# Instruction streams of TensorE, ScalarE and VectorE put in order by a list scheduler

## The reference

```python
for i in range(2):
    n = rms_norm(h, g_mix[i])
    h = h + (conv_pair_mixer(n, ...) if i % 2 == 0 else chunked_sgu_mixer(n, ...))
    mem_n = rms_norm(mem, g_mem[i])
    h = h + memory_cross_attention(rms_norm(h, g_xattn[i]), mem_n, ...)
    h = h + swiglu(rms_norm(h, g_ffn[i]), ...)      # (silu(n @ w_gate) * (n @ w_up)) @ w_down, width 2816
return rms_norm(h, g_final)
```

## Time and profile before

| | |
|---|---|
| median of 3 runs | 1797.18 us (1795.05 to 1807.06) |
| the profiled execution's own time | 1793.89 us |
| its span on the slowest core (core 3) | 1792.4 us; the eight cores 1776.1 to 1792.4 us |
| busy: PE, DVE, ACT | 90%, 56%, 38% of the span |
| mean granted TensorE clock | 0.972 of full speed on core 3 |
| DMA | 130.60 MB, 73 GB/s on the mean |

### The profile page before, as it was taken

The page is one execution under the profiler, slowest core; times in us unless marked ns, Lnnn a source line. Parts: engine busy times, 40 slices in busy tenths (PEclk is TensorE's granted clock), DMA queues, the critical chain, the costliest instruction groups (busy, mean ns, idle before and its releaser), DMA issues.

```text
span 1792.4 us, 23249 instructions; the slowest of 8 cores (1776.1 to 1792.4 us)
## 1 busy us (share of the span) xinstructions
PE 1614.3 (90%) x7650; PEld 732.0 (41%) x7650; DVE 998.7 (56%) x1602; ACT 687.5 (38%) x1153; POOL 70.6 (4%) x147
## 2 busy tenths in 40 slices
PE   3899868899999989899997797989989999989995
PEld 1344433444334434344443354444433444434442
DVE  1539654645774356663555762554777346673555
ACT  3522364454362132531434432354445133342242
POOL 1000000000000000000000001000000000000000
PEclk9899988999999999999998899999999999999998
DMA  9152537430145354443430209032023445364332
GB/s 227 51 95 36 83 57 179 72 59 1 22 73 82 55 93 76 81 73 71 88 69 16 47 1 153 13 71 48 1 48 65 77 74 103 71 164 82 74 70 94
DMA packets 32373, 130.60 MB, mean 73 GB/s; under 512 B 3584, under 2 KB 10112, under 8 KB 25472
## 3 DMA queue, kind: packets, MB, share of 16 engines
q0 software_dynamic: 18432, 100.03, 32.3%
q1 hardware_dynamic: 13824, 29.08, 5.5%
HBM read 216.51 MB, written 8.39 MB: 125 GB/s over the span
## 4 chain that ended last, share of the span: by engine, by line
PE 69%; DVE 12%; ACT 7%; issue 6%; DMA 5%; SPq 1%; DVEq 0%; ACTq 0%; POOLq 0%
PE ps L487 53%; PE ps L485 13%; PE ps L80 2%; ACT L80 1%; DMA hT_63<-x_in 1%; DVE sw L80 1%; DMA wbuf_185<-w_od_out 1%; DVE wd L80 1%; DVE t_3_62 L80 1%; DVE nT_68 L80 1%; DVE t_2_61 L80 1%; PE ps L909 1%; DVE hT_65 L80 1%; DVE w_0_94 L80 1%; DVE w_4_98 L80 1%
## 5 line engine op out<-in xcount | busy, mean ns | idle before, releaser
L487 PE MATMUL ps<-pT,VW 128*128 128x512 f16 x512 | 122.0, 387 | 4.0 <-DVE pT L80 4.0
L80 ACT ACTIVATE ps<-ps 128x512 f32<-128x512 f32 x88 | 47.7, 567 | 179.2 <-PE ps L487 178.6
L80 DVE TENSOR_TENSOR hT_63<-hT_63,ps 128x512 f32<-128x512 f32 x64 | 44.0, 688 | 113.3 <-PE ps L487 112.9
L487 PE MATMUL ps<-tw,sw 128*128 128x512 f16 x352 | 84.4, 382 | 6.7 <-DVE sw L80 4.4
L485 PE MATMUL ps<-tw,sw 128*128 128x512 f16 x352 | 86.0, 387 | 4.2 <-ACT ps L80 3.5
L80 ACT ACT_TABLE_LOAD x42 | 53.9, 1283 | 69.2 <-PE ps L80 29.4
L80 DVE TENSOR_TENSOR hT_64<-hT_64,ps 128x512 f32<-128x512 f32 x64 | 43.9, 686 | 62.4 <-PE ps L487 62.1
L487 PEld LDWEIGHTS ps<-pT,VW 128*128 128x128 f16 x512 | 50.8, 100 | 67.4 <-issue 9.8
L80 ACT ACTIVATE pT<-ps,epsc 128x512 f16<-128x512 f32 x64 | 43.7, 683 | 77.0 <-PE ps L487 76.4
L80 DVE TENSOR_TENSOR hT_66<-hT_66,ps 128x512 f32<-128x512 f32 x64 | 43.8, 685 | 49.6 <-PE ps L487 49.4
L80 DVE TENSOR_TENSOR hT_65<-hT_65,ps 128x512 f32<-128x512 f32 x64 | 43.9, 686 | 49.3 <-PE ps L487 49.1
(11 more groups left out here) (1236 smaller groups left out, 3372.3 us busy)
## 6 DMA issues: line engine op xcount, KB each, us to landing
hT_64<-x_in SPq DMA_DIRECT2D x8, 512.0 KB, 17.4
hT_65<-x_in SPq DMA_DIRECT2D x8, 512.0 KB, 20.3
hT_66<-x_in SPq DMA_DIRECT2D x8, 512.0 KB, 18.2
X<-a_ph SPq DMA_DIRECT2D x16, 130.0 KB, 6.0
hT_63<-x_in SPq DMA_DIRECT2D x4, 512.0 KB, 10.5
yA<-yst SPq DMA_DIRECT2D x32, 64.0 KB, 6.5
out<-hT_63 SPq DMA_DIRECT2D x4, 512.0 KB, 5.9
out<-hT_64 SPq DMA_DIRECT2D x4, 512.0 KB, 3.3
```

Of the source, the lines that this page charges most:

```text
L80: return self.add(eng, lambda e: getattr(e, meth)(**kw), reads, writes)
L487: ins = e.matmul(out, lhsT=l, rhs=r, start=(i == 0), stop=(i == np_ - 1))
```

## The change

Recording stays as it is. Each operation now carries an estimate of its cost (`_op_cost`, `_mm_cost`, bytes for a DMA). Before the semaphores are assigned, `schedule` plays the program through with these costs, a latency per engine from an operation's end to its users (LAT), and one shared link for all DMAs at 190 KB per us, plus 0.8 us ahead of a transfer and 1.2 us after it. Each engine has a window of its next operations in recorded order (AHEAD: 6 on PE, 10 on ACT, 12 on DVE, 1 on POOL and SP). Step by step the operation of any window that can start earliest is taken, the earlier recorded one where two are equal, and it is appended to the engine's new stream. POOL and SP, with a window of 1, keep their order. No operation is added or taken away. Dependencies are kept per operation (`after`) and cut to the last one per engine only after the new order is known. Neither a load of ACT's function tables nor TensorE's clock is in the costs.

```diff
--- before.py
+++ after.py
@@ -55,7 +55,29 @@
         self.dead = False
 
 class Op:
-    __slots__ = ("eng", "fn", "deps", "idx", "need_inc", "dma", "dma_val")
+    __slots__ = ("eng", "fn", "deps", "after", "idx", "need_inc", "dma", "dma_val", "cost", "done", "users", "left",
+                 "ready", "n")
+
+def _free(ap):
+    n = 1
+    for s in ap.shape[1:]:
+        n *= s
+    return n
+
+def _op_cost(eng, kw):
+    aps = [v for k, v in kw.items() if k in ("out", "in_", "in0", "in1", "rhs", "ap") and hasattr(v, "shape")]
+    n = max(_free(a) for a in aps)
+    if eng == "pe":
+        return _mm_cost(n)
+    if eng == "act":
+        return 0.19 + n / 1200
+    if eng == "dve":
+        half = all("16" in str(a.dtype) for a in aps)
+        return 0.155 + n / (1920 if half else 960)
+    return 0.1 + n / 600
+
+def _mm_cost(n):
+    return max(0.025, n / 2400 + 0.0025)
 
 class Ring:
     def __init__(self, items):
@@ -69,30 +91,36 @@
 
 class Prog:
     ENGS = ("pe", "act", "dve", "pool", "sp")
+    AHEAD = {"pe": 6, "act": 10, "dve": 12, "pool": 1, "sp": 1}
+    LAT = {"pe": 0.25, "act": 0.08, "dve": 0.08, "pool": 0.1, "sp": 0.1}
+    DMA_RATE = 190e3
     EPOCH = 500
 
     def __init__(self):
         self.streams = {e: [] for e in self.ENGS}
         self.dma_cnt = {}
         self.final_dma = set()
+        self.count = 0
 
     def op(self, eng, meth, reads=(), writes=(), **kw):
-        return self.add(eng, lambda e: getattr(e, meth)(**kw), reads, writes)
+        return self.add(eng, lambda e: getattr(e, meth)(**kw), reads, writes, cost=_op_cost(eng, kw))
 
     def dma(self, eng, sem, reads=(), writes=(), **kw):
-        return self.add(eng, lambda e: e.dma_start(**kw), reads, writes, dma=sem)
+        return self.add(eng, lambda e: e.dma_start(**kw), reads, writes, dma=sem, cost=kw["in_"].nbytes())
 
     def dma_part(self, eng, sem, slot, first, reads=(), **kw):
         prev = slot.w
-        o = self.add(eng, lambda e: e.dma_start(**kw), reads, [slot] if first else [], dma=sem)
+        o = self.add(eng, lambda e: e.dma_start(**kw), reads, [slot] if first else [], dma=sem, cost=kw["in_"].nbytes())
         if not first:
             assert prev.dma == sem
             slot.w = o
         return o
 
-    def add(self, eng, fn, reads=(), writes=(), dma=None):
+    def add(self, eng, fn, reads=(), writes=(), dma=None, cost=0.1):
         o = Op()
         o.eng, o.fn, o.dma, o.need_inc, o.idx, o.dma_val = eng, fn, dma, False, None, None
+        o.cost, o.done, o.users, o.n = cost, None, [], self.count
+        self.count += 1
         deps = {}
         for s in reads:
             assert not s.dead, s.name
@@ -109,25 +137,84 @@
                 for r in v.r.values():
                     deps[id(r)] = r
         for s in reads:
-            s.r[eng if dma is None else ("dma", id(o))] = o
+            s.r[id(o)] = o
         for s in writes:
             s.w = o
             s.r = {}
         deps.pop(id(o), None)
-        o.deps = []
-        for d in deps.values():
-            if d.dma is None and dma is None and d.eng == "pe" and eng == "pe":
-                continue
-            o.deps.append(d)
-            if d.dma is None:
-                d.need_inc = True
+        o.after = list(deps.values())
         if dma is not None:
             self.dma_cnt[dma] = self.dma_cnt.get(dma, 0) + 16
             o.dma_val = self.dma_cnt[dma]
         self.streams[eng].append(o)
         return o
 
+    def schedule(self):
+        heads = {e: [] for e in self.ENGS}
+        rest = {e: iter(self.streams[e]) for e in self.ENGS}
+        out = {e: [] for e in self.ENGS}
+        free = {e: 0.0 for e in self.ENGS}
+        link = 0.0
+        for e in self.ENGS:
+            for o in self.streams[e]:
+                o.left, o.ready = len(o.after), 0.0
+                for d in o.after:
+                    d.users.append(o)
+
+        def fill(e):
+            while len(heads[e]) < self.AHEAD[e]:
+                o = next(rest[e], None)
+                if o is None:
+                    return
+                heads[e].append(o)
+        for e in self.ENGS:
+            fill(e)
+        while True:
+            best = None
+            for e in self.ENGS:
+                for o in heads[e]:
+                    if o.left:
+                        continue
+                    t = max(free[e], o.ready)
+                    if best is None or (t, o.n) < best[:2]:
+                        best = (t, o.n, e, o)
+            if best is None:
+                break
+            t, _, e, o = best
+            heads[e].remove(o)
+            out[e].append(o)
+            if o.dma is None:
+                free[e] = t + o.cost
+                o.done = free[e] + self.LAT[e]
+            else:
+                free[e] = t + (0.6 if e == "pool" else 0.1)
+                link = max(link, t + 0.8) + o.cost / self.DMA_RATE
+                o.done = link + 1.2
+            for u in o.users:
+                u.left -= 1
+                u.ready = max(u.ready, o.done)
+            fill(e)
+        assert all(len(out[e]) == len(self.streams[e]) for e in self.ENGS)
+        self.streams = out
+        return max(free.values())
+
     def assign(self):
+        for e in self.ENGS:
+            for i, o in enumerate(self.streams[e]):
+                o.n = i
+        for e in self.ENGS:
+            for o in self.streams[e]:
+                last = {}
+                for d in o.after:
+                    if d.dma is None and o.dma is None and d.eng == "pe" and e == "pe":
+                        continue
+                    key = d.eng if d.dma is None else ("dma", id(d))
+                    if key not in last or last[key].n < d.n:
+                        last[key] = d
+                o.deps = list(last.values())
+                for d in o.deps:
+                    if d.dma is None:
+                        d.need_inc = True
         neps = {}
         for e in self.ENGS:
             c = 0
@@ -486,7 +573,8 @@
                 else:
                     ins = e.matmul(out, lhsT=l, rhs=r, start=(i == 0), stop=(i == np_ - 1))
             return ins
-        o = self.P.add("pe", fn, reads=reads, writes=[self.ps_s[b]])
+        o = self.P.add("pe", fn, reads=reads, writes=[self.ps_s[b]],
+                       cost=sum(_mm_cost(_free(r)) for _, r in pairs))
         self.tick(np_ / KC)
         return o
 
@@ -631,7 +719,7 @@
                     ins = e.matmul(self.ps[b][:, i * NMEM:(i + 1) * NMEM], lhsT=ws[i][0](k), rhs=mn[:, k, :],
                                    start=(k == 0), stop=(k == KC - 1))
             return ins
-        P.add("pe", fn, reads=ws[0][1] + ws[1][1] + list(mn_s), writes=[self.ps_s[b]])
+        P.add("pe", fn, reads=ws[0][1] + ws[1][1] + list(mn_s), writes=[self.ps_s[b]], cost=16 * _mm_cost(NMEM))
         self.tick(1)
         P.op("act", "activation", [self.ps_s[b]], dst_s[2 * mp:2 * mp + 2],
              out=dst[:, 2 * mp:2 * mp + 2, :].rearrange("p m n -> p (m n)"), in_=self.ps[b][:, :], func=AF.Copy)
@@ -856,7 +944,7 @@
                         ins = e.matmul(ps[:, cc * 128:(cc + 1) * 128], lhsT=self.v_ln[tt][:, cc, g * 128:(g + 1) * 128],
                                        rhs=self.w_sT[:, g, :], start=True, stop=True)
                     return ins
-                P.add("pe", fn, reads=self.v_ln_s[tt] + [self.w_sT_s], writes=[self.ps_s[bs]])
+                P.add("pe", fn, reads=self.v_ln_s[tt] + [self.w_sT_s], writes=[self.ps_s[bs]], cost=4 * _mm_cost(128))
                 bu = self.linear(self.wc("od_in", 0, g), KC, lambda k: self.nT[tt][:, k, :], self.nT_s[tt], TT)
                 ug = self.t32.next()
                 P.op("act", "activation", [self.ps_s[bu]], [ug.slot], out=ug.t[:, :], in_=self.ps[bu][:, :],
@@ -910,7 +998,7 @@
                                        lhsT=w(c), rhs=self.kT[:, c, :],
                                        start=(hc == 0), stop=(hc == 1))
                 return ins
-            P.add("pe", fn, reads=ws + self.kT_s[4 * hp:4 * hp + 4], writes=[self.ps_s[b]])
+            P.add("pe", fn, reads=ws + self.kT_s[4 * hp:4 * hp + 4], writes=[self.ps_s[b]], cost=4 * _mm_cost(NMEM))
             self.tick(1)
             evict(b, self.G[:, d, hp * 512:(hp + 1) * 512], self.G_s[d])
 
@@ -1179,6 +1267,7 @@
         assert not self.reserved, self.reserved
         dma_names = sorted(self.P.dma_cnt.keys())
         with ExitStack() as st:
+            self.P.schedule()
             neps = self.P.assign()
             esem = {(e, i): st.enter_context(nc.semaphore(f"s_{e}{i}")) for e in Prog.ENGS for i in range(neps[e])}
             dsem = {n: st.enter_context(nc.semaphore("d_" + n)) for n in dma_names}
```

## The result

The changed kernel takes 1729.57 us, the median of 4 runs (1728.17 to 1750.04), against 1796.12 us for the kernel before, run beside it (1793.98 to 1807.06). The ratio is 0.9644, with a 95% interval of 0.9563 to 0.9726: 3.6% faster. I had forecast 1735 us in a range of 1702 to 1776. Some executions show cores at a lower granted clock than the others; where they would decide a comparison, the text names the executions or cores that are compared.

The account below looks back on a forecast made before the run. TensorE was taken as the bound, busy 1614.3 of 1792.4 us, with its waits to win. Gains 39 + 8 + 14 + 5 + 3 + 2.3 less costs 5 + 3 + 1 gave 62.3 us: 1735 us predicted, range 1702 to 1776.

Parts of the forecast that it names:

- The FFN: Both FFN layers: regular waits, sums waiting for a slab and seams mended, 39 us together, between 15 and 56.
- the regular wait: FFN pairs: the second copy stands behind a waiting Silu on ACT, 0.53 us in each of 43; 22 us taken.
- The rest: FFN seams where norm jobs lie between pairs: half of 27 us mended, 13 us, between 5 and 27.
- Table loads: ACT: other functions get between a norm's Ln and Exp; 4 splits, half on the path, cost 5 us, 0 to 41.
- Rival (1): ACT: all 16 places split, whole cost on TensorE's path, 41 us in place of 5: 1771; chance 0.08.
- G: Scores of both layers: two waits for G, 9.0 us, mended as the copy goes first; 8 us, between 4 and 9.
- Second mixer: Slab 174 wait partly filled, 5.24 us ones-matmul stall gone, clock loss regained: 14 us, low end 5; 8.9 us wait stays.
- First norms and short convolution: Norms end sooner, 5 us (0 to 6); waits for b_ph in the short convolution shrink, 3 us (0 to 7.7).
- Costs of filling: TensorE: a group taken as filler delays one ready just after by up to 1.73 us; costs 3 us, 0 to 10.
- (2): FFN not mended: ACT on time in both modelled orders, or another operation is late instead; 1774, chance 0.08.
- (3): Whole kernel: nothing moves, gains given back at waits that stay, such as slabs and yA; about 1793, chance 0.08.
- (4): DVE: weight sums put too early block its stream until slabs land; slower, 1830 with 35 slabs; chance 0.08.

Follow-up runs that it names:

- experiment 1: The kernel before, no scheduler, with the Silu of an FFN pair's first Y buffer recorded behind the second buffer's copy: 1768.31 us, ratio 0.9835.
- experiment 7: The changed kernel with a switch of ScalarE's function table priced at 1.3 us in the scheduler: 1704.20 us, ratio to before 0.9433.
- Experiment 12: The kernel of experiment 7, with copies of G going first where modelled starts are equal: 1694.92 us, ratio to before 0.9408.
- experiment 9: The kernel of experiment 7, with all 16 copies of G on ScalarE, where 8 went to VectorE: 1698.2 us.
- Experiment 6: The changed kernel with TensorE's look-ahead cut from six entries to one: 1726.89 us.
- experiment 10: The kernel of experiment 7, with DMA transfers reckoned at 400 in place of 190 KB per us: 1703.7 us.
- experiment 8: The changed kernel with table loads priced at 1.3 us and TensorE kept in recorded order: 1728.21 us over all eight cores.

## Why the prediction was right, and which terms were off

**The FFN (39 us taken, 15 to 56).** Measured 24.6 + 24.1 = 48.7 us. The step is right: copies ahead of the Silu, 12.09 us a pair, the 43 waits gone, and experiment 1 shows by itself what the regular wait is worth, 29.6 us for the 22 I took. I had sized it by the one pair of the earlier trace rows, with 0.36 us of idle time and 0.17 us of slower matmuls behind it. By the earlier trace rows the 43 waits are 27.7 us; without the two long ones (3.4 and 3.2 us) 0.51 us each, so 41 x 0.68 = 28 us. That is an estimate from rows of before, and experiment 1 agrees with it. Nor is 48.7 all: in experiment 7, where the loads are kept together, the FFNs take 419.1 and 419.5 us, 66.8 us less than before. "The rest" of the FFN, which I halved to 13 us since the norm jobs' own work would stay, is mendable in full. The 66.8 us are more than TensorE's idle time there (48.6 us), since the matmuls behind a wait were slower too: TensorE's busy time in the first FFN falls from 426.92 us to 419.10.

**Table loads (5 us taken, 0 to 41).** I expected 4 splits of 16 places, "half of it on the path". There are three, and as the count of loads rose by 2 only, the new order saves four loads at other places. What I had wrong is the price of a split where TensorE stands right behind it: 1.25 us by my sum, but at 714.53 it is a wait of 3.51 us (two loads and the Silu between them are 3.2 us of ScalarE's time) and 1.44 us of slower matmuls. The two splits in the FFNs cost about 10 us by this (an estimate from these rows and those at 1515.73); what the third cost is not shown. Pricing the loads gives back 25 us, 18 of them in the FFNs, but that is more than the splits: with 38 loads it is a better order than the recorded one, which had 42 and split no norm. Rival (1), all 16 places split, did not occur. The rule of the Trainium skill ("ScalarE: Activation LUTs", Table sets: the hidden batching unit) to batch activations by set is borne out by this. The price of 2.66 us that the Trainium skill gives for a switch ("ScalarE: Activation LUTs", What ACT_TABLE_LOAD costs) is not: from load to activation it is 709.37 - 708.07 = 1.30 us here too, and the load begins as the copy ahead of it ends (707.46 + 0.60 us), so no drain shows on either side.

**G (8 us taken, 4 to 9).** The waits fell from 4.48 to 3.50 us each, 2 us, and the two new ones of 1.9 us just ahead take that back: 9.0 us before, 8.9 after. "In the new order the copy goes first" is the step that failed. Where two entries can start at once, the earlier recorded one goes, and the scales of the third tile are recorded earlier. Experiment 12 makes the copy go first, and then the 9 us are there; experiment 9 shows that taking VectorE out of it is not enough, since eleven copies in a row on ScalarE are as long a queue.

**Second mixer (14 us taken, from 5).** 10.2 us. The wait for slab 174 is 4.1 us in place of 7.4, where I had filled all but 2.2; the 5.24 us stall is gone, but the layer norm's chain is late next, by 2.24 us at 971.82; and the 8.9 us, which I had down as fixed, fell to 5.1 us, as TensorE found chunk mixing to do first. Experiment 6 shows whose work this is: without TensorE's window the stretch up to the chunk mixing is 8 us longer.

**First norms and short convolution (5 and 3 us taken).** 1.5 us together. The waits for b_ph fell from 7.7 to 2.0 us, but the norms gained nothing that is clear of the spread: five table loads from 45.64 to 55.29 us, one pair of them around a Sigmoid between Ln and Exp, hold ScalarE. With loads priced (experiment 7) the stage ends 9.5 us earlier than before, all that I took and more.

**The end (2.3 us taken).** 2.7 us. TensorE's last wait, for a sum of squares on VectorE, is 3.52 us in place of 9.16, and the scales follow each other.

**Costs of filling (3 us) and yA (1 us).** yA's wait grew from 17.8 to 19.0 us. The fillers' cost is at the place that the table shows with a plus, before the scores of layer 1: TensorE waits 1.35 us twice (at 1075.02 and 1080.51) for column sums put ahead of ready groups, since slabs are modelled late; experiment 10 removes both. Without TensorE's window (experiment 6) that stretch is 6 us shorter; part of the other 3 us are shorter waits for G (4.5 us in both layers, 8.9 after).

**The other rivals.** (2) is refuted by the pair. (3), that waits only change their names, holds for TensorE's window beside the other two, where its gains and losses cancel (experiment 6). (4), sums put too early, did not occur: no row of VectorE waits for a slab's DMA any more, slab 147 (10.4 us to landing) included. Slower was possible, but by another way than (4): a look-ahead for TensorE alone, 21 us.

**Luck.** The main step was right, but that the forecast is only 5 us off is luck in part: the FFN brought 10 us more than I took, loads included, while G fell short by 8 us, the second mixer by 4, and the first norms with the short convolution by 6.5.

## What to carry to other kernels

A static list scheduler is as good as what its costs leave out: price the switch of function tables, and check by the trace where modelled landings and real ones part. Give the look-ahead to the engines that empty the banks first; in this kernel TensorE's own was worth 0 to 5 us beside a better order of its producers, and cost 1% without it. Break ties by who waits for the result, not by the order of recording.

## What I had not expected of the hardware

Beside the two levels of 1.2 and 2.4 GHz (0.50 and 1.00) the granted clock has stretches at 0.81. In the profiled run of experiment 8 core 1 was at 0.81 from 912 to 1071 us, but for 7 us at 0.50 behind a second slab wait of 8.55 us. This began 8 us after a slab wait of 7.99 us had ended, and ended among the short waits of 1060 to 1080 us. Core 0 had 0.81 at the same places. The other six cores waited 6.99 to 9.56 us at the same step, and their clock was 0.99 or 1.00 from 920 to 960 us: the long wait alone does not bring it.

Nor is a long wait needed. In experiment 1 cores 0 and 1 both fell to 0.81 at 644 us, after TensorE had been busy throughout from 635 to 643 us, while cores 2 and 3 stayed at 1.00; cores 1 and 2:

```profile
645.00:658.00 13.00, 13.00 (x51) 0.81 0.43 70
...
645.00:658.00 13.00, 13.00 (x62) 1.00 0.33 55
```

In all eight cores of that trace the stretches at 0.81 lie at the same times in pairs of neighbours (0 and 1, 2 and 3, 4 and 5, 6 and 7). What starts them stays open.
